# Expert rows added onto the output by accumulating DMAs, with a sixth weight buffer, in the expert stage of a decoder block

## What is computed

```python
# x: the residual after the mixing sub-layer; h = modulate(rmsnorm(x)); gt_f: the gate
g_idx = argmax(h @ w_rg + b_rg)              # one of 4 groups
top_w, top_i = top_k(softmax(e_logits in that group), 2)
top_w = top_w / sum(top_w) * p_g             # a token's two shares
for e in range(32):
    hid = silu(h @ w_e_gate[e]) * (h @ w_e_up[e])
    ffn = ffn + combine[:, e:e+1] * (hid @ w_e_down[e])
out = x + gt_f * ffn
```

## Time and profile before

| | |
|---|---|
| median of 3 runs | 1576.92 us (1576.4 to 1578.83) |
| profiled execution, its time | 1577.04 us |
| its span | 1575.2 us |
| PE busy | 1389.8 us, 88% |
| DVE / ACT / POOL busy | 768.5 / 496.0 / 257.8 us |
| HBM read / written | 216.12 / 38.29 MB |

### The profile page before, as it was taken

One profiled execution on the slowest core, in us unless ns is written; L12 is line 12 of the kernel. 1 busy time (PEld: TensorE's weight loads), 2 busy tenths in 40 slices (PEclk: granted clock), 3 DMA queues, 4 the chain that ended last, 5 costly groups with the idle time before them and its releaser, 6 DMA issues. The chain is left out here.

```text
span 1575.2 us, 32797 instructions
## 1 busy us (share of the span) xinstructions
PE 1389.8 (88%) x14309; PEld 996.4 (63%) x14309; DVE 768.5 (49%) x1095; ACT 496.0 (31%) x906; POOL 257.8 (16%) x301
## 2 busy tenths in 40 slices
PE   3799999976999998799988999998994899999990
PEld 0597777734899988677766888786883433333330
DVE  0644866756666664544656555555435211211215
ACT  1543332353344443444544445222111111111110
POOL 0001222205556542011110000000000111111110
PEclk7899999996999999899998999999996799999995
DMA  9841222270000020650021113414018599999958
GB/s 357 295 138 47 81 74 74 67 268 2 4 4 4 4 64 4 177 198 14 15 92 69 54 54 135 173 40 154 39 40 338 218 355 413 414 420 411 410 220 322
DMA packets 80636, 246.54 MB, mean 157 GB/s; under 512 B 8680, under 2 KB 41960, under 8 KB 63728
## 3 DMA queue, kind: packets, MB, share of 16 engines
q1 hardware_dynamic: 73152, 227.69, 38.9%
q0 software_dynamic: 7344, 16.79, 2.8%
HBM read 216.12 MB, written 38.29 MB: 162 GB/s over the span
## 5 line engine op out<-in xcount | busy, mean ns | idle before, releaser
L2807 PE MATMUL ps<-gu,xT 128*32 128x512 f32 x1536 | 175.9, 599 | 1.4 <-ACT xT L2888 0.7
L2807 PEld LDWEIGHTS ps<-gu,xT 128*32 128x32 f32 x1536 | 47.7, 111 | 106.3 <-issue 102.3
L3022 DVE TENSOR_TENSOR sg<-sg,ps 128x256 f32<-128x256 f32 x25 | 10.5, 422 | 211.2 <-ACT sg L2893 211.2
L351 PE MATMUL ps<-hh,wr_h 128*128 128x512 f32 x224 | 93.1, 416 | 0.6 <-DVE wr_l L347 0.6
L352 PE MATMUL ps<-hl,wr_h 128*128 128x512 f32 x224 | 88.5, 395 | 0.0
L353 PE MATMUL ps<-hh,wr_l 128*128 128x512 f32 x224 | 88.4, 395 | 0.0
L2825 PE MATMUL ps<-dn,hidT 128*32 128x512 f32 x768 | 86.8, 592 | 0.5 <-ACT hidT L2897 0.5
L2016 DVE TENSOR_REDUCE nmax<-ps 128x1 f32<-128x896 f32 (+4 forms) x64 | 45.8, 753 | 71.2 <-PE ps L1914 70.6
L1402 DVE TENSOR_TENSOR inverses<-inverses,ps 128x512 f32<-128x512 f32 (+1 forms) x80 | 49.9, 631 | 62.2 <-PE ps L1625 61.9
L1187 POOL TENSOR_TENSOR off<-mats,cst 128x256 f32<-128x256 f32 x80 | 65.8, 839 | 56.6 <-PE ps L1609 56.5
L1625 PE MATMUL ps<-inverses,xx 64*64 64x64 f32 x1280 | 71.2, 218 | 0.0
(11 more groups left out here) (411 smaller groups left out, 3338.5 us busy)
## 6 DMA issues: line engine op xcount, KB each, us to landing
gu<-w_e_gate SPq DMA_DIRECT2D x34, 1024.0 KB, 12.8
gu<-w_e_up SPq DMA_DIRECT2D x34, 1024.0 KB, 15.3
dn<-w_e_down SPq DMA_DIRECT2D x34, 1024.0 KB, 11.6
wbuf<-w_ada SPq DMA_DIRECT2D x16, 1024.0 KB, 11.4
wbuf<-w_ada SPq DMA_DIRECT2D x16, 512.0 KB, 6.1
wraws<-w_gates SPq DMA_DIRECT2D x16, 512.0 KB, 4.9
rows<-expert_rows SPq DMA_DIRECT2D x16, 512.0 KB, 9.3
wr<-w_rwkv SPq DMA_DIRECT2D x14, 512.0 KB, 3.6
```

The costliest lines, as they stand in the source:

```text
L351: nc.tensor.matmul(out, wt[0], mov[0], start=(k == 0), stop=False)
L2807: last = nc.tensor.matmul(ps[part, GB[b]], xT[:, b, k, part], gu[:, expert(m, c_) % WB, :, k], start=(k == 0), stop=(k == KD - 1))
```

## The change

It does four things.

1. Before the expert stage each tile of `x1` is stored to the output (`x1_out`). DVE scales a pass's rows by gate and share at once, and POOL adds them onto the output in DRAM with indirect accumulating DMAs. `expert_rows`, the reading back, the final adds and the final stores are gone.
2. Two accumulates onto one token's row must not overlap. The two rows of a token are therefore sorted by slot: what was "first expert" and "second expert" becomes "lower slot" and "higher slot", with their shares. Each pass is sent in two transfers, the tokens' first rows and their second rows, with the other rows skipped by index. The second transfer of a pass waits until the first has landed; so each token's second row comes after its first, in whatever pass that was.
3. The shares for each pass and row come out of the same matrix product as the indices, whose right side is twice as wide.
4. `WB` becomes 6. The sixth buffer and `gt` lie where `x1` was, so SP waits for `x1_out` before it loads set 5. The index copies now stand ahead of the overflow table on DVE.

```diff
-WB = 5
+WB = 6
...
                     sp.dma_start(h2_v[t], h2[:, t % 3]).then_inc(h2_out[t % 3], 16)
+                    sp.dma_start(out_v[t], x1[:, t]).then_inc(x1_out, 16)
...
                 for e in range(1, WB):
+                    if e == WB - 1:
+                        sp.wait_ge(x1_out, 16 * NT)
                     load_gate_up(e)
                     load_down(e)
...
+                def add(col, buf, done):
                     pool.indirect_dma_start(
+                        out=out[0], out_offset=bass.IndirectOffsetOnAxis(ap=col.bitcast(u32), axis=0),
                         in_=yo[:, buf], in_offset=None,
+                        bounds_check=SEQ - 1, oob_is_err=False, compute_op=ALU.add).then_inc(done, 16)
+
+                def add_first(j):
+                    pool.wait_ge(y_ev, 2 * j + 2)
+                    if j == 0:
+                        pool.wait_ge(home_s, 3)
+                        pool.wait_ge(x1_out, 16 * NT)
+                    add(home[:, j, 0:1], j % YSLOTS, first_out[j % YSLOTS])
+
+                def add_second(j):
+                    pool.wait_ge(first_out[j % YSLOTS], 16 * (j // YSLOTS + 1))
+                    add(home[:, j, 1:2], j % YSLOTS, second_out[j % YSLOTS])
                 clear_signals_of_last_phase(pool)
                 pool.wait_ge(h2_s, NT)
+                pool.wait_ge(lmm, NT)
...
                     fetch(idx[:, m:m + 1], m % XSLOTS)
-                    if m == XSLOTS:
-                        pool.wait_ge(home_s, 1)
-                    if m >= XSLOTS + 2:
-                        j = m - XSLOTS - 2
-                        pool.wait_ge(y_ev, 2 * j + 2)
-                        send(home[:, j:j + 1], j % YSLOTS)
+                    j = m - XSLOTS - 2
+                    if j >= 1:
+                        add_second(j - 1)
+                    if j >= 0:
+                        add_first(j)
                 for j in range(FIXED - XSLOTS - 1, FIXED):
-                    pool.wait_ge(y_ev, 2 * j + 2)
-                    send(home[:, j:j + 1], j % YSLOTS)
+                    add_second(j - 1)
+                    add_first(j)
+                add_second(FIXED - 1)
+                for b in range(YSLOTS):
+                    pool.wait_ge(second_out[b], 16 * (FIXED // YSLOTS))
                 n = steps(pool)
...
+                    add(now[:, 1:2], 0, first_out[0])
+                    pool.wait_ge(first_out[0], i * 16 + (16 * (FIXED // YSLOTS) + 16))
+                    pool.sem_inc(chosen, 1)
+                    add(now[:, 2:3], 0, second_out[0])
...
-                        m = nc.tensor.matmul(ps[:, IDX, 0:NPASS + 2], row_is[:, i, t], block_is[:, i, t],
+                        m = nc.tensor.matmul(ps[:, IDX, 0:2 * (NPASS + 2)], row_is[:, i, t],
+                                             block_is[:, i, t].rearrange("p a n -> p (a n)"),
...
                 slot, block = m1[:, 0:2], m1[:, 2:4]
+                link(V.tensor_tensor(rowp[:, 0], slot[:, 0], slot[:, 1], ALU.is_lt))
+                link(V.tensor_tensor(m1[:, 2], slot[:, 0], slot[:, 1], ALU.min))
+                link(V.tensor_tensor(slot[:, 1], slot[:, 0], slot[:, 1], ALU.max))
+                link(V.tensor_copy(slot[:, 0], m1[:, 2]))
+                link(V.tensor_scalar(rowp[:, 1], rowp[:, 0], -1.0, 1.0, ALU.mult, ALU.add))
+                kept = [homef[:, i, a * NT:(a + 1) * NT] for i in range(2) for a in range(2)]
+                for i, (share_, if_) in enumerate(((0, 0), (1, 1), (0, 1), (1, 0))):
+                    link(V.tensor_tensor(kept[i], top[:, share_], rowp[:, if_], ALU.mult))
+                for i in range(2):
+                    link(V.tensor_tensor(top[:, i], kept[2 * i], kept[2 * i + 1], ALU.add))
...
+                    V.tensor_tensor(shares_of, rows_of, top[:, i].unsqueeze(2).broadcast_to([P, NT, NPASS + 2]), ALU.mult)\
+                     .then_inc(one_s, 1)
...
-                        nc.vector.tensor_tensor(yo[:, buf, cols], ps[:, 6 + half], gt[:, cols], ALU.mult)\
-                          .then_inc(y_ev, 1)
+                        nc.vector.scalar_tensor_tensor(yo[:, buf, cols], ps[:, 6 + half], share_, gt[:, cols],
+                                                       ALU.mult, ALU.mult).then_inc(y_ev, 1)
+
+                def fixed_rows_out(m):
+                    if m >= YSLOTS:
+                        dve.wait_ge(second_out[m % YSLOTS], 16 * (m // YSLOTS))
+                    rows_out(m, m % YSLOTS, share[:, m:m + 1])
```

More of the change, by code:

```diff
@@ L2064, in build @@
         yr = alias("yr7", [P, NT, D])
+        with ExitStack() as st:
+            gu_last, dn_last = sb(st, "gu_last", [P, 2, KD, FE]), sb(st, "dn_last", [P, 2, D])
+            gt_ffn = sb(st, "gt9", [P, D])
         x1 = sb(xst, "x1", [P, NT, D])
+        out_v = out[0].rearrange("(t p) d -> t p d", p=P)
         with phase() as st:
@@ L2618, in build @@
             idx = sb(st, "idx", [P, NPASS + 2], i32)
-            home = sb(st, "home", [P, NPASS + 2], i32)
+            home = sb(st, "home", [P, NPASS + 2, 2], i32)
             homef = sb(st, "homef", [P, 2, NPASS + 2])
[L2621 to L2624, removed]
+            share = sb(st, "share", [P, NPASS + 2])
+            now = sb(st, "now", [P, 3], i32)
+            now_share = sb(st, "now_share", [P, 1])
+            dn = [sb(st, f"dn{w}", [P, 2, D]) for w in range(WB - 1)] + [dn_last]
+            gu = [sb(st, f"gu{w}", [P, 2, KD, FE]) for w in range(WB - 1)] + [gu_last]
             xg = sb(st, "xg", [P, XSLOTS, D])
@@ L2679, in load_gate_up @@
                     for half, view in enumerate((wg_v, wu_v)):
[L2680 removed]
+                        sp.dma_start(gu[e % WB][:, half], view[:, e]).then_inc(gu_in[e % WB], 16)
                 def load_down(e):
[L2683 removed]
+                    sp.dma_start(dn[e % WB][:], wd_v[:, e]).then_inc(dn_in[e % WB], 16)
                 sp.wait_ge(o_mm, NT)
@@ L2825, in fixed_down @@
                                 last = nc.tensor.matmul(ps[part, 6 + half], hidT[:, b, k, part],
-                                                        dn[:, expert(m, c_) % WB, k, half * 512:(half + 1) * 512],
+                                                        dn[expert(m, c_) % WB][:, k, half * 512:(half + 1) * 512],
                                                         start=(k == 0), stop=(k == 1))
@@ L2837, in gate_up @@
                             part = slice(UNIT * b, UNIT * (b + 1))
-                            last = nc.tensor.matmul(ps[part, GB[0]], xT[:, 0, k, part], gu[:, OVER_W[b], :, k],
+                            last = nc.tensor.matmul(ps[part, GB[0]], xT[:, 0, k, part], gu[OVER_W[b]][:, :, k],
                                                     start=(k == 0), stop=(k == KD - 1))
@@ L2913, in _ @@
                     act.sem_inc(turned, 1)
-                act.wait_ge(y_out[0], n * 16 + 16 * (FIXED // YSLOTS))
+                act.wait_ge(second_out[0], n * 16 + 16 * (FIXED // YSLOTS))
                 act.sem_inc(turned, 1)
-                for b in range(1, YSLOTS):
-                    act.wait_ge(y_out[b], 16 * (FIXED // YSLOTS))
-                act.sem_inc(all_out, 1)
             @block.vector
@@ L3025, in hidden, with rows_out @@
                       .then_inc(hid_s, 1)
-                def rows_out(m, buf, count):
-                    if count is not None:
-                        dve.wait_ge(y_out[buf], count)
+                def rows_out(m, buf, share_):
                     for half in range(2):
```

88 lines of the change are left out of this document (36 added, 52 removed).

## The result

| | before | after |
|---|---|---|
| median | 1576.66 us (4 runs, 1576.12 to 1578.83) | 1597.92 us (4 runs, 1595.3 to 1601.6) |
| profiled execution, span | 1577.04, 1575.2 us | 1597.22, 1595.4 us |

The ratio is 1.0134, with an interval of 1.0111 to 1.0157: **slower by 1.3%**. Forecast were 1562.4 us and a range up to 1583. The direction is wrong, and the time lies outside the range.

The account below looks back on a forecast made before the run. PE and the DMA engines were taken as both full in the passes, DMA 0.9 us short per three passes. Span 1575.2 - 24.2 (end) + 3.25 (routing) + 2.8 (first fetch) + 3.5 (accumulates) = 1560.55, hence 1562.4 us; range 1554 to 1583.

Parts of the forecast that it names:

- Pass 0 begins: Start of the expert passes: routing adds 3.25 us, the first fetch behind the sixth buffer's loads 2.8 us.
- the wait on `lmm` ahead of POOL's memset: Before pass 0: hidden by the wait for the indices, so it costs nothing.
- Rival (a): POOL's chain of adds in the passes becomes the bound, up to 1619 us at a landing of 14; chance 0.16.
- part one: After the last pass: reading, adding and storing disappear, two accumulates run one after the other; 24.2 us less.
- What an accumulate costs the engines: DMA engines in the passes: an accumulate costs twice a scatter's 0.87 us, giving 3.5 us of waiting.
- The tail: Last pass: its fetch stands behind POOL's last adds and landing waits, so the tail is 5.5 us late.
- The end: After DVE's last output: landings of 2.8 us each for two accumulates, then 0.5 us to close.
- (b): DMA engines in the passes: accumulates cost three scatters, 1575.4 us, around no change; chance 0.15.
- (c): DMA engines in the passes: accumulates cost no more than scatters, 1558.9 us; chance 0.18.
- (d): Sixth set held back by its wait for the x1 stores, first fetch loses nothing; 1571.4 us, chance 0.04.

Follow-up runs that it names:

- swapped kernel: The changed kernel with add_first(j) issued ahead of add_second(j - 1) in both loops of POOL's list; 1578.29 us, ratio 1.0017 to the kernel before.
- best version: Changed kernel with adds swapped, the loop's first fetch ahead of add_first(22), and the sixth set loaded after pass 0's transposes; 1566.63 us, ratio 0.9918.

## Why the prediction was wrong

Its span was 1560.55, measured were 1595.4: 34.9 us more. The swapped kernel splits them, 20.3 for the order of the adds and 14.6 for the rest.

- **Pass 0 begins.** The time is right, 1243.52 against 1243.5, but that is luck: the router's last matmuls began at 1197.06 here and at 1198.36 in the trace of before, in stages that differ only by the stores of `x1` (in the eleven traces it is 1196.79 to 1202.32). Counted from there pass 0 came 7.4 us later, not 6.05. The fetch was issued 3.7 us later instead of 3.25 and took 8.3 us until the transposes, 3.7 more than before instead of 2.8. The product's 32 matmul halves of twice the columns took 7.12 us against 7.06, so doubling them cost 0.1, not 0.4. What the forecast put at nothing, and was not, is the wait on `lmm` ahead of POOL's memset. Timelines of POOL and DVE, before and then after:

```profile
1195.71 2.66 POOL L2728 MEMSET xg<- 128x3072 f32 x1 [377.55 <-DVE YTM L2602]
1203.56 0.29 DVE L2944 COPY each<-each 128x256 f32<-128x256 f32 x1
```

```profile
1200.82 2.66 POOL L2748 MEMSET xg<- 128x3072 f32 x1 [383.71 <-PE ps L2284]
1202.25 1.37 DVE L2969 COPY each<-each 128x256 f32<-128x256 f32 x1
```

The later memset runs into a copy of DVE's routing. The copy takes 1.36 or 1.37 us in all nine kernels with that wait, and ends 0.15 us after the memset; it takes 0.29 in the two without. That is 1.1 us ahead of pass 0. No run moves the memset by itself, so the cause is argued from the two times.
- **The landing and its chain: the step that failed.** Rival (a) described the mechanism: POOL issues the first add, waits, issues the second and only then the next pass's first. Its period was put at L + 1.3, fitting while L is below 10.5, from scatters that landed in 8.9 us. Measured: L + 2.65 (0.77 to wake up, 1.58 for the issue, 0.30 between), fitting while L is below 9.1, and an L of 11.1. Both halves of the comparison were short, by 1.35 and by 2.2 us, and together they turn 10.2 against a pass of 11.77 into 13.7. The wake-up was even in the forecast, as 0.8 us in part one, and left out of (a)'s period. So the forecast's sum has nothing for POOL in the passes, where it fell 2.0 us behind PE with each. The price of (a) came near: 22 passes at 2.0 us over, less the 25 us that POOL is ahead, make some 18 us (an estimate), and the swap was worth 20. That the kernel came out 1.3% slower took the other 14.6 us as well; without the chain it would still have missed the forecast, by 16 us. What was wrong in (a) was its chance of 0.16: the sum took the accumulate as two scatters for the engines, but the landing as one scatter's for POOL.
- **What an accumulate costs the engines.** Right: twice. The stall of 3.5 us that followed from it, with 14.0 of 17.5 us covered, was 5.0 us of waiting in the swapped kernel, and 7.5 with the half clock behind the wait, which the term did not have.
- **The tail.** 5.5 us late by the forecast, whose own numbers give 5.8 (6.2 less the 0.39 for which PE had waited for `hid`). The swapped kernel, where POOL is not behind, was 11.5 late: the transposes came 8.2 us late instead of 6.2, and PE then ran at the 1.2 GHz level, which the term did not have. In the changed kernel it was 24.5.
- **The end.** 7.7 us by the forecast, 12.5 measured, and 12.2 to 12.5 in every other kernel that adds onto the output. The first add landed after 2.74 us as forecast; the second, of the same pass, after 4.6 (forecast 2.8), and the span closed 3.4 us after that (forecast 0.5, which was the kernel before's, whose last DMAs came from SP).
- **Rivals.** (b) fell, adding costs two scatters and not three. (c) fell with it. (d) fell: the sixth set was loaded early, early enough to cost the first fetch 3.6 us.

What the parts are worth, then: the removed end gave 24.9 us; routing and fetch took 7.4 of them; the doubled work 7 or 8 in the passes; the tail 11.5 unless its fetch is moved; and the order of the adds 20. With order, tail and sixth set mended the kernel is 0.8% faster than before, and the forecast's own sum, without its tail, is 1557; the best version's 1566.6 is above it by the end's 4.8, by 3.3 in the listed passes (its waits for weights and the half clock behind them) and by 1.6 at the start of pass 0, where the stages ahead of routing had ended later.

Open is why an adding transfer's issue takes 1.55 us on POOL instead of 1.0, and how much of its landing's 1.0 us is that issue and how much the doubled work; no run took these apart. Every kernel that adds onto the output keeps the order between a token's two adds, so what goes wrong without it is not shown. The kernel with the early fetch and the late sixth set was not run with fewer than six buffers.

## What to carry to other kernels

When an asynchronous step is turned into issue, wait, issue on one engine's list, write out that engine's whole period (landing, wake-up, each issue, each gap) and set it against the bound's period; a chain that fitted by 1.6 us on paper (10.2 of 11.77) was 2.0 over in the run. If it comes near, put the next item's independent issue ahead of the wait before anything else is tuned: here two swapped lines were worth 20 us. A term that is doubled for one resource has to be doubled, or argued, for every other that sees the same operation.

## What the runs showed of the hardware

- The issue of an adding indirect DMA kept POOL busy for 1.55 us, that of the same transfer without the add for 0.98.
- A transfer that goes out right behind another one lands later: in the kernel without adding and with swapped order, the first of each pair took 8.4 us in the median, the second, 1.3 us behind it, 10.1 (1300 to 1500).
- Of two adding transfers one after the other on idle engines, the first landed after 2.74 us and the second after 4.6; the span ended 3.4 us after the last landing. In the kernel before, whose last DMAs are SP's stores, it ended 0.4 us after the last landing.
- A wait of 4.22 us in the middle of a busy stretch let the granted clock fall to 0.50, and the next 32 matmuls took 6.12 us instead of 3.62. In the changed kernel waits of 2.30 and 3.11 us were followed by transposes of 1.97 us for eight, as against 1.06, and by 32 matmuls of 4.14 and 4.35 us; after one of 3.19 us the transposes took 1.16 and the matmuls behind them ran slowly (granted clock 0.52 from 1502.6 to 1505). For the price of a stall, the clock behind it counts too.
- A fetch that meets a full load queue took 8.1 to 9.5 us, into a draining one 4.6 to 4.9.
- A DVE copy of 128x256 took 1.37 us while POOL's memset ran, and 0.29 when it had ended before.
